# Products in front of a residual, token tile by token tile, in an encoder step on one Trainium2 core

## What is computed

```python
def rmsnorm(x, g):
    xf = x.astype(jnp.float32)
    y = xf * lax.rsqrt(jnp.mean(xf * xf, axis=-1, keepdims=True) + EPS)
    return (y * g.astype(jnp.float32)).astype(x.dtype)

def swiglu(h, i, W):
    return (jax.nn.silu(h @ W['w_ffn_gate'][i]) * (h @ W['w_ffn_up'][i])) @ W['w_ffn_down'][i]

        h = rmsnorm(x, g[0]) * (1 + sc1) + sh1
        ...
        x = x + gt1 * rmsnorm(y, g[1])
        h = rmsnorm(x, g[2]) * (1 + sc2) + sh2
        x = x + gt2 * rmsnorm(swiglu(h, i, W), g[3])
```

## Time and profile before

| | us |
|---|---|
| median of 3 runs | 3556.11 (3551.8 to 3559.77) |
| span of the profiled execution, first to last instruction | 3540.5 |
| TensorE busy | 3220.4 (91%) |
| TensorE weight loads busy | 2904.5 (82%) |
| DVE busy | 1218.8 (34%) |
| ScalarE busy | 1037.2 (29%) |
| GpSimd busy | 155.4 (4%) |
| mean granted clock of TensorE | 0.922 of full |

### The profile page before, as it was taken

One profiled execution on the slowest core, in us unless ns is written; L12 is line 12 of the kernel. 1 busy time (PEld: TensorE's weight loads), 2 busy tenths in 40 slices (PEclk: granted clock), 3 DMA queues, 4 the chain that ended last, 5 costly groups with the idle time before them and its releaser, 6 DMA issues.

```text
span 3540.5 us, 53095 instructions
## 1 busy us (share of the span) xinstructions
PE 3220.4 (91%) x18909; PEld 2904.5 (82%) x18909; DVE 1218.8 (34%) x2578; ACT 1037.2 (29%) x2090; POOL 155.4 (4%) x197
## 2 busy tenths in 40 slices
PE   6999988888679999999949999999994999999997
PEld 4655587787679999999948878788694999999996
DVE  3333333332442232323472222222227232323326
ACT  4322233333241111122243333333224212121123
POOL 2000000000100000000020000000002000000000
PEclk9999988877889999999969999999596999999998
DMA  9444212211101111111121111111020111111111
GB/s 307 134 138 135 89 34 26 26 19 69 36 24 38 51 42 51 45 39 57 36 75 47 41 38 38 38 38 38 13 85 12 42 47 43 52 33 56 48 33 64
DMA packets 279679, 201.65 MB, mean 57 GB/s; under 512 B 25932, under 2 KB 270356, under 8 KB 279156
## 3 DMA queue, kind: packets, MB, share of 16 engines
q1 hardware_dynamic: 271748, 166.31, 16.9%
q0 software_dynamic: 7792, 33.43, 2.8%
HBM read 181.49 MB, written 23.44 MB: 58 GB/s over the span
## 4 chain that ended last, share of the span: by engine, by line
PE 87%; DVE 6%; ACT 2%; issue 2%; DVEq 1%; DMA 1%; POOL 0%; SPq 0%; ACTq 0%; POOLq 0%
PE psum L679 22%; PE psum L680 21%; PE psum L681 21%; PE psum L824 6%; PE psum L770 5%; PE psum L850 5%; PE psum L838 3%; DVE x L1600 2%; DVE norm_buf L1557 1%; DVE diag L1548 1%; DVEq L1610 1%; ACT w_hi L1110 1%; PE psum L738 1%; PE psum L950 1%; PE psum L951 1%
## 5 line engine op out<-in xcount | busy, mean ns | idle before, releaser
L679 PE MATMUL psum<-h_hi,w_hi 128*128 128x352 f32 x3240 | 1081.4, 334 | 47.2 <-DVE w_lo L1496 19.1
L681 PE MATMUL psum<-h_hi,w_lo 128*128 128x352 f32 x3240 | 1053.0, 325 | 2.6 <-issue 2.6
L680 PE MATMUL psum<-h_lo,w_hi 128*128 128x352 f32 x3240 | 1053.4, 325 | 1.9 <-issue 1.9
L679 PEld LDWEIGHTS psum<-h_hi,w_hi 128*128 128x128 f32 x3240 | 620.0, 191 | 79.3 <-issue 31.0
L680 PEld LDWEIGHTS psum<-h_lo,w_hi 128*128 128x128 f32 x3240 | 621.6, 192 | 7.6 <-issue 7.6
L681 PEld LDWEIGHTS psum<-h_hi,w_lo 128*128 128x128 f32 x3240 | 619.3, 191 | 2.8 <-issue 2.8
L1496 DVE TENSOR_TENSOR w_lo<-w_raw,w_hi 128x1024 fp32r<-128x1024 f32 x231 | 282.2, 1224 | 698.1 <-ACT w_hi L1110 698.1
L679 PE MATMUL psum<-ff_hi,w_hi 128*128 128x352 f32 x1056 | 342.5, 324 | 3.9 <-DVE w_lo L1496 3.6
L1110 ACT ACTIVATE w_hi<-w_raw 128x1024 fp32r<-128x1024 f32 x231 | 242.5, 1053 | 353.6 <-PE psum L681 342.3
L680 PE MATMUL psum<-ff_lo,w_hi 128*128 128x352 f32 x1056 | 341.9, 324 | 0.0
L681 PE MATMUL psum<-ff_hi,w_lo 128*128 128x352 f32 x1056 | 341.9, 324 | 0.0
(11 more groups left out here) (307 smaller groups left out, 3547.3 us busy)
## 6 DMA issues: line engine op xcount, KB each, us to landing
ada_m<-in_w_ada SPq DMA_DIRECT2D x40, 1024.0 KB, 5.2
w_raw<-in_w_ffn_gate SPq DMA_DIRECT2D x88, 192.0 KB
w_raw<-in_w_ffn_up SPq DMA_DIRECT2D x88, 192.0 KB
w_raw<-in_w_ffn_down SPq DMA_DIRECT2D x112, 128.0 KB
w_raw<-in_w_in_c SPq DMA_DIRECT2D x48, 192.0 KB
x<-x_spill POOLq DMA_DIRECT2D x2, 4224.0 KB, 12.8
ada_s<-in_w_ada SPq DMA_DIRECT2D x8, 1024.0 KB, 11.3
w_raw<-in_w_ffn_down SPq DMA_DIRECT2D x128, 64.0 KB
```

Source lines behind the costliest of these rows:

```text
L679: nc.tensor.matmul(out, w_hi[:, slot, k], hi[:, k, c], start=(k == 0), stop=False)
L680: nc.tensor.matmul(out, w_hi[:, slot, k], lo[:, k, c], start=False, stop=False)
L681: last = nc.tensor.matmul(out, w_lo[:, slot, k], hi[:, k, c], start=False, stop=(k == kt - 1))
```

## The change

The products in front of a residual run with token tiles outside and weight tiles inside: 24 visits (VISITS), each one weight tile and one token tile. Every weight tile is loaded and split three times. While a token tile is multiplied, the residual and the next norm of the token tile before it are issued between the visits, by `chain(n, v)` on TensorE, ScalarE and DVE. Token tile 2 has no tile behind it: its steps stand in the first FFN group (`entries`, ten entries of a gate and an up tile for one or two token tiles, 20 weight tiles instead of 8) or in the first q and k products. In the last FFN the output blocks 0 to 4 stand between the visits too. The groups are 4, 4, 4, 4, 6, so the last down products have six inner tiles. `project` does all products with `w_hi` first, waiting for the high part alone, and then those with `w_lo`. `turn` orders the diagonals' two buffers for the new order, and the output buffers lie elsewhere.

```diff
-FF_GROUPS = [5, 5, 4, 4, 4]
+FF_GROUPS = [4, 4, 4, 4, 6]
+
+ENTRIES = [(0, (0,)), (1, (0,)), (0, (1,)), (1, (1,)), (2, (0, 1)), (3, (0, 1)), (0, (2,)), (1, (2,)), (2, (2,)), (3, (2,))]
...
             def out_tiles(layer):
                 g0 = plan[f"out{layer}"][0]
                 w = view(I["w_out_c"][0]) if layer else None
+                for tt in range(NTT):
+                    with sp.Fori(0, KD // 2) as j:
+                        for par in range(2):
+                            slot = (g0 + par) % 2
+                            c = bass.ds(j * 256 + par * 128, 128)
...
+            def project(g, slot, tt, hi, lo, kt, b, free, part=None, count=1):
+
+                out = psum[:, b, 0:TW]
+                c = tt_cols(tt)
+                if part is None:
+                    pe.wait_ge(free[0], free[1])
+                    pe.wait_ge(hi_done, g + 1)
+                    for k in range(kt):
+                        nc.tensor.matmul(out, w_hi[:, slot, k], hi[:, k, c], start=(k == 0), stop=False)
+                        nc.tensor.matmul(out, w_hi[:, slot, k], lo[:, k, c], start=False, stop=False)
+                    pe.wait_ge(lo_done, g + 1)
+                    for k in range(kt):
+                        last = nc.tensor.matmul(out, w_lo[:, slot, k], hi[:, k, c], start=False, stop=(k == kt - 1))
+                    last.then_inc(proj_done, count)
+                    return
...
-                pe.wait_ge(acc_done, 24 * (n // 2) + 18 + 2 * tt + 2 + CREDIT)
+                pe.wait_ge(acc_done, 24 * (n // 2) + 8 * (tt + 1) + CREDIT)
...
+            def chain(n, v):
+
+                tt, s_ = v // KD, v % KD
+                if tt >= 1 and s_ == 1:
+                    sum_y(n, tt - 1)
+                if tt >= 1 and s_ == 2:
+                    spread(n, tt - 1)
+                if tt >= 1 and s_ == 7 and n < 7:
+                    sum_x(n + 1, tt - 1)
+                if tt == 2 and s_ == 0 and n < 7:
...
+            def y_block(b):
+
+                m = qrows(b)
+                pe.wait_ge(x_new, 9 + (128 * b + m - 1) // TW + 1)
+                behind = 1 if b >= 6 else 0
+                if b >= 1:
+                    pe.wait_ge(yt_read, b - behind)
+                for k in range(KD):
...
-                with pe.Fori(0, KD // 2 - 1) as j:
-                    for par in range(2):
-                        act_tile(f"out{layer}", j * 2 + par, (g0 + par) % 2, (o_hi, o_lo))
-                last_pair(1 + 4 * layer, lambda s_, tt, par: project(
-                    g0 + KD - 2 + par, (g0 + par) % 2, tt, o_hi, o_lo, KD, s_ % 3, (evac_act, a0 + 3 * (KD - 2) + CREDIT - 2 + s_)))
+                n = 1 + 4 * layer
+                for v in range(VISITS):
+                    chain(n, v)
+                    project(g0 + v, (g0 + v) % 2, v // KD, o_hi, o_lo, KD, v % 3, (evac_act, a0 + CREDIT - 2 + v), count=3)
...
+            def entries(layer):
+                g0, _, a0, d0 = plan[f"gu{layer}0"]
+                n = 1 + 4 * layer
+                u = 0
+                for e, (f, tts) in enumerate(ENTRIES):
+                    for half in range(2):
+                        if (e, half) in ((0, 0), (5, 0)):
+                            spread(n + 1, 1 if e == 0 else 2)
+                        if (e, half) == (0, 1):
+                            sum_y(n, 2)
+                        if (e, half) == (1, 0):
+                            spread(n, 2)
+                        if (e, half) == (4, 1):
+                            sum_x(n + 1, 2)
+                        for i, tt in enumerate(tts):
+                            pe.wait_ge(hl_done, 3 + 6 * layer + tt + 1)
+                            free = (evac_act, a0 + CREDIT + u + i - 1) if half == 0 else (evac_dve, d0 + CREDIT + u + i - 1)
+                            project(g0 + 2 * e + half, (g0 + half) % 2, tt, h_hi, h_lo, KD, 2 * half + (u + i) % 2, free,
+                                    count=3 if len(tts) == 1 else i + 1)
+                    u += len(tts)
 
             def ffn(layer):
                 for n, ff in enumerate(FF_GROUPS):
                     g0, _, a0, d0 = plan[f"gu{layer}{n}"]
                     if n == 0:
...
+                        for v in range(VISITS):
+                            chain(3 + 4 * layer, v)
+                            if layer == 1 and v in (13, 14, 21, 22, 23):
+                                y_block({13: 0, 14: 1, 21: 2, 22: 3, 23: 4}[v])
+                            pe.wait_ge(fflo_done, nff)
+                            project(g0 + v, (g0 + v) % 2, v // KD, ff_hi, ff_lo, ff, v % 3, (evac_dve, d0 + CREDIT - 2 + v), count=3)
+                        continue
...
+            spread(4, 1)
             for s_, (tt, i) in enumerate(PAIR):
+                if s_ == 1:
+                    sum_y(3, 2)
+                if s_ == 2:
+                    spread(3, 2)
+                if s_ == 4:
+                    sum_x(4, 2)
+                    spread(4, 2)
...
-                    act.wait_ge(proj_done, u + (3 * g0 + 1))
-                    dst = y_mix[:, bass.ds(tile, 1) if not isinstance(tile, int) else slice(tile, tile + 1), tt_cols(tt)]
-                    A(dst.rearrange("p o c -> p (o c)"), bank(b_, TW), ACT.Copy)
-                    act.wait_ge(acc_done, u + (48 * layer + 1))
+                n = 1 + 4 * layer
+                for v in range(VISITS):
+                    tt, b_ = v // KD, v % 3
+                    split_hi(g0 + v + 2, (g0 + v) % 2)
+                    act.wait_ge(proj_done, 3 * (g0 + v + 1))
+                    A(y_mix[:, v % KD, tt_cols(tt)], bank(b_, TW), ACT.Copy)
...
+            def chain(n, v):
+
+                tt, s_ = v // KD, v % KD
+                if 1 <= tt <= 2 and s_ == 1:
+                    root(n, tt - 1)
+                if n == 7:
+                    return
+                if 1 <= tt <= 2 and s_ == 5:
+                    square(n + 1, tt - 1)
+                if 1 <= tt <= 2 and s_ == 7:
+                    root(n + 1, tt - 1)
+                if tt == 2 and s_ == 1:
+                    if n == 1:
+                        act.wait_ge(derived, 2)
+                    affine((n + 1) // 2, 0)
+                if tt == 2 and s_ == 2:
+                    high((n + 1) // 2, 0)
...
+                for e, (f, tts) in enumerate(ENTRIES):
+                    if e == 0:
+                        root(n, 2)
+                    if e == 5:
+                        affine(i_h, 2)
+                    split_hi(g0 + 2 * e + 2, g0 % 2)
+                    for i, tt in enumerate(tts):
+                        act.wait_ge(proj_done, 3 * (g0 + 2 * e) + (3 if len(tts) == 1 else 1 + 2 * i))
+                        act.wait_ge(evac_dve, d0 + CREDIT + u)
+                        A(sil[:, tt_cols(tt)], bank((u + i) % 2, TW), ACT.Silu).then_inc(evac_act, 1)
+                    if e == 0:
+                        affine(i_h, 1)
+                    if e == 3:
+                        square(n + 1, 2)
+                    if e == 4:
+                        root(n + 1, 2)
+                    if e == 5:
+                        high(i_h, 2)
+                    split_hi(g0 + 2 * e + 3, (g0 + 1) % 2)
+                    if e == 0:
+                        high(i_h, 1)
+                    for i, tt in enumerate(tts):
+                        act.wait_ge(evac_dve, d0 + CREDIT + u + i + 1)
+                        A(ff_hi[:, f, tt_cols(tt)], ffs[:, tt_cols(tt)], ACT.Copy).then_inc(ffhi_done, 1)
+                    u += len(tts)
 
...
+                    act.wait_ge(acc_done, v + (24 + 48 * layer + 1))
+                    A(sq_ring[v % 3][:, :], y_ffn[:, v % KD, tt_cols(v // KD)], ACT.Square).then_inc(sqy_done, 1)
+                    chain(3 + 4 * layer, v + 1)
+                    if layer == 1 and v in (13, 14, 21, 22):
+                        y_block({13: 0, 14: 1, 21: 2, 22: 3}[v])
...
+            def chain(n, v, src):
+
+                tt, s_ = v // KD, v % KD
+                if 1 <= tt <= 2 and s_ == 1:
+                    inverse(n, tt - 1)
+                if 1 <= tt <= 2 and s_ == 2:
+                    rms(n, tt - 1, src)
                     dve.drain()
-                    ahead = [(n, tt + 1)] if tt < NTT - 1 else [(n + 1, 0)] if more else []
-                    for p in ahead:
-                        mean_square(*p)
-                    add(tt, 0)
-                    for p in ahead:
-                        diagonals(*p)
-                    add(tt, 1)
-                if not more:
...
+                    add_square(v, (evac_act, v + (a0 + CREDIT + 1)), v % 3, v // KD)
                     dve.drain()
+                    chain(1 + 4 * layer, v + 1, y_mix)
...
+                u = 0
+                for e, (f, tts) in enumerate(ENTRIES):
+                    if e == 0:
+                        rms(n + 1, 1, x).then_inc(xn_done, 1)
+                        inverse(n, 2)
+                    if e == 1:
+                        rms(n, 2, y_mix)
```

(25 more changed lines are left out.)

424 lines of the change are left out of this document (192 added, 232 removed).

## The result

| | kernel before | changed kernel |
|---|---|---|
| median of the runs, us | 3557.45 (3551.8 to 3559.77, 4 runs) | 3580.91 (3565.65 to 3588.49, 4 runs) |
| profiled execution, span, us | 3540.5 | 3564.0 |
| ratio | | 1.0063, 95% interval 1.0036 to 1.0091 |

The changed kernel is slower by 0.6%, 23.5 us between the two profiled executions. Forecast were -14 us, 3542, with a range of 3495 to 3590: the time lies inside the range, the sign was wrong.

A forecast was written before the change was run, and what follows sets the result against it. TensorE, busy 91% of 3540.5 us, was taken as the bound, with four residual pauses costing 249 us. Terms: -249 + 43 + 43 + 81 + 71 - 3 = -14 us, span 3526, median 3542, range 3495 to 3590.

The forecast's parts named there:

- Stretch 2: Last down projection, second residual and start of qkv: forecast to cost 81 us where it cost 66, so slower.
- stretch 4: Last down projection of the second layer to the end: forecast to cost 71 us where it cost 45.
- first inner group: First FFN group behind each out projection, where token tile 2 finishes residual and norm: 22 us lost.
- Reloading x (4.2 MB) runs beside three weight loads ... 0 to 4 us, I take 1: Out projections: loading x back beside the weight loads costs TensorE 0 to 4 us, taken as 1.
- Products now wait for the high part alone ... the rest give 3: Shorter waits for the low part of the weights, outside the replaced stretches, gain 3 us.
- so these 2.91 and 3.81 are no cost: Visits of 2.91 us (down projection) and 3.81 us (out projection) add nothing, as the number of product matmuls is unchanged.
- the folds: GpSimd folds of x's squares, 6.2 us each: TensorE waits 3.0 and 5.5 us for the sums in out projections.
- stretch 1: First out projection and first inner group: forecast to cost 43 us where it cost 69.
- stretch 3: Out projection and first inner group of the second layer: forecast to cost 43 us where it cost 69.
- Low clock in the chains: Rival: visits 9 to 23 and first inner entries mostly run at 1.2 GHz; +57 us, 3599; chance 0.20.
- Loads become the bound: Rival: a load takes 5 us instead of 3.3, +36 us for 48 down-projection visits, 3578; chance 0.08.
- The waits close up: Rival: queues overlap, folds and blocks go, stretches cost 30, 30, 60, 55; -77 us, 3479; chance 0.13.

The follow-up runs named there:

- the spaced reload: Changed kernel with x loaded back in six 0.7 MB pieces, two visits apart, in the out projections; ratio 1.0039 to the kernel before.

## Why the prediction was wrong

**What held.** The reading of the kernel before (four pauses with 249 us in them) and the mechanism: the chain is cut in pieces, and each piece makes an in-order queue wait at one known place. Stretch 2 was forecast 15 slower and was 16.4, stretch 4 26 and 26.7, with the errors inside them that are told above. Of the waits shown above, eleven of twelve came within 2 us; the chain of token tile 2 in front of qkv ended 51.9 us after the last down product (1803.5 to the end of its low part at 1855.4), forecast 51.6. That TensorE waited 28.5 us there and not the forecast 7.8 + 26.1 = 33.9 is because the work in front of it was longer: TensorE was busy for 23.4 us there and not 17.7, at a mean granted clock of 0.69. The "first inner group" was forecast at 22 over its 91.9 us and took 113.8.

**The step that failed first: "Reloading x (4.2 MB) runs beside three weight loads ... 0 to 4 us, I take 1".** It cost 5.4 us of pause and 2.3 of clock in each of the out projections: 6.7 more than taken, 13 in both. The price of a load (3.3 us) was read from the earlier trace rows, in a down projection where the DMA share was 0.26, and applied to a place where a transfer of 4.2 MB stands in front. The trace of before held the answer, for x landed there 12.8 us after its issue by the page; it stood hidden under a weight tile that lasted three visits. When a change cuts the time for which a tile lasts to a third, every transfer beside it has to be asked how long it holds the queue.

**The second: "Products now wait for the high part alone ... the rest give 3", and before it "so these 2.91 and 3.81 are no cost".** A visit was taken as 24 products of a fixed length in any order. The order alone costs +5.1 us in the loops of the kernel before, and +10.0 stood there in the changed kernel, with the 2 x 2.0 us behind the group of six: 13 off. The waits for the low part did shrink (TensorE was idle for 4.7 us less in the run with the order alone), but most lay in stretches that the change replaced. The forecast saw that part.

**The third, smaller:** the folds held TensorE for 3.7 and 7.5 us in the out projections instead of 3.0 and 5.5. They took longer than the 6.21 us of the earlier trace rows, for a reason below. With the slower products in 48 visits (0.03 each, 1.6 us) the three make 6.7 + 2.7 + 1.6 = 11.0 in stretch 1, where 12.0 were missing, and 11.3 in stretch 3, where 10.0 were: what is left over, a microsecond up or down, is the other terms.

**The rivals.** "Low clock in the chains" would have been 3599 (two thirds of its 88 us are 59 and not 57, so rather 3601). The time went a good part of that way, but not by its mechanism. The lower clock took 61.4 us of TensorE's busy time in the four stretches and 49.8 before, 11.6 more. The forecast itself had 19 more in it (34 against 15), so its clock terms were too large and not too small. "Loads become the bound" named the queue that was late, at the wrong place and by the wrong cause: its 36 us were to come from the down projections, where ScalarE waits for no load at all (its waits there are for products and for DVE), and the spaced reload shows that the number of loads is no limit. "The waits close up" did not happen.

**The chances.** With 0.48 for faster and 0.35 for slower the text was near even, and the time was within its range, though outside the 3517 to 3567 that had 0.55. What it lacked was a rival for the loops, the part of the kernel that holds a third of its time and that was taken as unchanged because its instruction counts were.

## What to carry to other kernels

When a chain is cut up and laid under a loop, the walk through the queues gives its waits to a microsecond or two; what it misses is what it holds constant. Before trusting such a sum, ask of each transfer beside the loop how long it holds the DMA engines against the time that one tile now lasts, and measure one pass of an inner loop whose instructions were only put in another order: 0.9% of the gate/up groups made 5.1 us in the loops, over a third of the gain that was forecast. And leave work where it is free: the output blocks cost 22 us more inside the products than in and behind a wait that was there anyway.

## What the hardware showed

- **The order of products.** With alternating high, high and low weights a gate/up visit is 3.82 us, with sixteen of the high part and then eight of the low part 3.86, all at full clock and without waits. A down pass of four tiles takes 46.55 and 46.29 at the old address, 45.81 and 46.29 at the new one. No run here shows why.
- **An address.** Moving the low part of the activations by one row of 4224 bytes per partition made the down products 1.6% and the gate/up products 0.2% faster in the old order, and moved nothing in the new. Also without a cause that a run shows.
- **DVE beside GpSimd.** While the fold runs on GpSimd (909.47 to 916.5), DVE's instructions on SBUF operands take 2.8 and 3.8 times as long, here a weight split (1.22 us elsewhere) and an accumulation of squares (0.52 elsewhere):

```profile
910.36 3.41 DVE L1590 TENSOR_TENSOR w_lo<-w_raw,w_hi 128x1024 fp32r<-128x1024 f32 x1 [2.29 <-ACT w_hi L1169]
913.70 1.99 DVE L1686 TENSOR_TENSOR sil<-sil,sq_ring 128x352 f32<-128x352 f32 x1
```

  And the fold is slower too, 8.43 us with DVE beside it where the earlier trace rows have 6.21:

```profile
954.41 8.43 POOL L557 TENSOR_TENSOR norm_buf<-norm_buf 128x1408 f32<-128x1408 f32 x3 [37.95 <-ACT norm_buf L1194]
```

  In the kernel before the folds ran in the pauses, but the price can be read there too: the four additions of DVE that take 2.06 us in the earlier trace rows take 6.60 beside the fold of the earlier trace rows, which runs from 956.29 to 962.50. The forecast took each duration as the same wherever the instruction stands.

```profile
956.78 6.60 DVE L1600 SCALAR_TENSOR_TENSOR x<-norm_buf,post_gate,x 128x352 f32<-128x352 f32 x4
```

  The Trainium skill says it, in SBUF — State Buffer (Who interferes with whom): a DVE instruction with two inputs in SBUF contends with a GpSimd instruction that reads SBUF, for a pair of ports that only one of them can hold. The trace agrees, instruction by instruction: the split issued at 910.36 ends at 913.77, 1.08 us behind the fold's first instruction (912.69), and the fold's second, issued at 912.76, ends at 915.30, 1.53 us behind the split. ScalarE's split of 912.86 beside them keeps its 1.06.
